# A two-layer GLA and Mamba-2 trunk on one core: 512-column feature products, y before B's and C's convolution, the skip term on ScalarE

## What is computed

```python
proj = h @ w_in
z, xbc, dt = split(proj, [2048, 2048 + 4096])
xbc = silu(conv1d(xbc, conv_w, 4 taps, causal) + conv_b)
x, B, C = split(xbc, [2048, 2048 + 1024])
dt = softplus(dt + dt_bias)
y = y_diag + y_off + d_skip * x      # inside a chunk, from the state, and the skip term
y = y * silu(z)
y = rmsnorm(y by group) @ w_out
```

## Time and profile before

| | us |
|---|---|
| median of 3 runs | 1087.08 (1086.83 to 1087.44) |
| the profiled execution, its own time | 1086.96 |
| its span, first to last instruction | 1085.2 |
| PE busy | 1075.1 (99%) |
| DVE busy | 787.6 (73%) |
| ACT busy | 652.8 (60%) |
| POOL busy | 87.2 (8%) |
| mean granted clock of PE, as a share of full speed | 0.998 |

### The profile page before, as it was taken

One profiled execution on the slowest core, in us unless ns is written; L12 is line 12 of the kernel. 1 busy time (PEld: TensorE's weight loads), 2 busy tenths in 40 slices (PEclk: granted clock), 3 DMA queues, 4 the chain that ended last, 5 costly groups with the idle time before them and its releaser, 6 DMA issues.

```text
span 1085.2 us, 17549 instructions
## 1 busy us (share of the span) xinstructions
PE 1075.1 (99%) x6399; PEld 940.1 (87%) x6399; DVE 787.6 (73%) x1122; ACT 652.8 (60%) x1002; POOL 87.2 (8%) x138
## 2 busy tenths in 40 slices
PE   9999999999999999999999999999999999999997
PEld 7888888899888888888888888899999988888886
DVE  5867667785677666667766767889888888776664
ACT  7645446784676445458454447697777797454453
POOL 3000000011010000000000000153222211000000
PEclk9999999999999999999999999999999999999999
DMA  9864655375357555474655554595555536655531
GB/s 283 296 230 156 206 180 145 107 241 183 121 163 245 193 190 197 155 233 140 232 192 193 177 171 121 173 289 184 187 155 155 170 121 213 238 171 195 196 112 40
DMA packets 162881, 199.30 MB, mean 184 GB/s; under 512 B 6372, under 2 KB 145856, under 8 KB 162832
## 3 DMA queue, kind: packets, MB, share of 16 engines
q1 hardware_dynamic: 160288, 190.86, 53.9%
q0 software_dynamic: 2384, 7.72, 2.1%
q10 hardware_dynamic: 160, 0.08, 0.0%
HBM read 197.56 MB, written 1.08 MB: 183 GB/s over the span
## 4 chain that ended last, share of the span: by engine, by line
PE 92%; ACT 3%; DMA 2%; DVE 2%; issue 1%; SPq 0%; POOL 0%; DVEq 0%; ACTq 0%; POOLq 0%
PE ps L1772 27%; PE ps L1934 24%; PE ps L1948 13%; PE ps L1826 9%; PE ps L1835 6%; PE ps L1738 5%; PE ps L1859 4%; DMA raw<-in_ffn_w_up 1%; PE ps L1798 1%; PE ps L2294 1%; PE ps L2153 0%; ACT exps L882 0%; PE ps L2298 0%; DVE xres L1179 0%; PE ps L1757 0%
## 5 line engine op out<-in xcount | busy, mean ns | idle before, releaser
L1224 DVE TENSOR_TENSOR ws<-raw,ws 128x1024 fp32r<-128x1024 f32 x180 | 213.3, 1222 | 139.7 <-ACT ws L685 139.7
L1772 PE MATMUL ps<-ws,hT 128*128 128x512 f32 x1320 | 314.0, 392 | 0.0
L685 ACT ACTIVATE ws<-raw 128x1024 fp32r<-128x1024 f32 x183 | 184.7, 1053 | 173.2 <-PE ps L1948 160.3
L1772 PEld LDWEIGHTS ps<-ws,hT 128*128 128x128 f32 x1320 | 243.7, 188 | 49.5 <-issue 1.1
L1934 PE MATMUL ps<-xT,ws 128*128 128x512 f32 x1152 | 267.3, 389 | 0.2 <-ACT ws L685 0.2
L1934 PEld LDWEIGHTS ps<-xT,ws 128*128 128x128 f32 x1152 | 216.1, 188 | 45.5 <-ACT ws L685 0.6
L1146 DVE TENSOR_TENSOR ws<-raw,ws 128x2048 fp32r<-128x2048 f32 (+1 forms) x88 | 197.2, 2243 | 27.8 <-ACT ws L599 27.8
L599 ACT ACTIVATE ws<-raw 128x2048 fp32r<-128x2048 f32 x83 | 157.6, 1909 | 2.6 <-PE ps L1772 2.6
L1948 PEld LDWEIGHTS ps<-xT,ws 128*128 128x128 f32 x1152 | 142.6, 192 | 2.5
L1948 PE MATMUL ps<-xT,ws 128*128 128x256 f32 x1152 | 144.1, 283 | 0.0
L1826 PE MATMUL ps<-xT,ws 128*128 128x256 f32 x960 | 119.2, 284 | 0.0
(11 more groups left out here) (263 smaller groups left out, 864.3 us busy)
## 6 DMA issues: line engine op xcount, KB each, us to landing
raw<-in_ffn_w_down SPq DMA_DIRECT2D x88, 512.0 KB, 4.8
raw<-in_ffn_w_gate SPq DMA_DIRECT2D x86, 512.0 KB, 4.0
raw<-in_ffn_w_up SPq DMA_DIRECT2D x86, 512.0 KB, 5.0
raw<-in_ssd_w_in SPq DMA_DIRECT2D x48, 512.0 KB, 4.7
raw<-in_gla_w_in SPq DMA_DIRECT2D x24, 512.0 KB, 4.8
raw<-in_ssd_w_out SPq DMA_DIRECT2D x16, 512.0 KB, 4.3
raw<-in_gla_w_out SPq DMA_DIRECT2D x8, 512.0 KB, 5.5
exps<-cs_rows POOLq DMA_DIRECT2D x8, 512.0 KB, 5.1
```

The lines of the kernel that those rows point to most:

```text
L685: act.activation(ws[:, 0:2, 0, c], raw[:, 0:2, c], ACT.Copy).then_inc(gu_hi, 1)
L1224: dve.tensor_tensor(ws[:, 0:2, 1, c], raw[:, 0:2, c], ws[:, 0:2, 0, c].bitcast(F32), ALU.subtract).then_inc(gu_lo, 1)
L1772: mm = pe.matmul(ps[:, 2 * t + n, :], hT[:, par, j, a, t * P:(t + 1) * P], ws[:, slot, b, off:off + 512], start=(first and j + a + b == 0) ...
```

## The change

For groups 2 to 7 of the SSD mixer the products of P1 and P2 with the high weights take the high and the low tokens in one instruction of 512 columns (`wide_tiles`), so a bank holds two halves; ACT copies 512 columns into a buffer (`halves`) and DVE adds the halves into `feat` (`join`). The skip term `dx` is made by four ACT copies with a scale (`skips`) in steps 1 to 8, and POOL's two instructions go. In steps 2 to 6 DVE computes y ahead of the convolution of B and C, and ACT squares y ahead of their silus. The state's copy follows its product more closely in steps 2 and 7. At the ends of both mixers POOL's two instructions become eight, and ACT copies two blocks of xT ahead of one square. In step 7 DVE makes the low part of the output weights whole, which before lay half in step 7 and half in step 8.

```diff
+        halves = [scr[:, 1, o:o + 512] for o in (512, 1536)]
...
-                if not (isinstance(g, int) and g == 1):
-                    pool.wait_ge(y_out, 2 * (g - 1 + G))
-                for t in range(NT):
-                    pool.tensor_tensor(out=by_head(dx)[:, t], in0=by_head(xtok)[:, t],
-                                       in1=hb[:, 1, hs].rearrange("p (h o) -> p h o", o=1).broadcast_to([P, HPG, HD]),
-                                       op=ALU.mult).then_inc(tok_mul, 1)
...
-                    for c in (slice((NQ - 2) * QW, (NQ - 1) * QW), slice((NQ - 1) * QW, NQ * QW)):
-                        pool.tensor_tensor(ws[:, 0:2, 1, c], raw[:, 0:2, c], ws[:, 0:2, 0, c].bitcast(F32),
-                                           op=ALU.subtract).then_inc(gu_lo, 1)
+                    for q in range(NQ - 2, NQ):
+                        for o in range(0, QW, QW // 4):
+                            c = slice(q * QW + o, q * QW + o + QW // 4)
+                            ins = pool.tensor_tensor(ws[:, 0:2, 1, c], raw[:, 0:2, c], ws[:, 0:2, 0, c].bitcast(F32),
+                                                     op=ALU.subtract)
+                        ins.then_inc(gu_lo, 1)
...
+            def halves_out(slot, count, banks, done, earlier, columns=(0, 1)):
+                for c in columns:
+                    act.wait_ge(tile_mm[slot], count * 2 + c + 1)
+                    if earlier is not None:
+                        act.wait_ge(joined, earlier + c + 1)
+                    act.activation(halves[c], ps[:, banks + c, :], ACT.Copy).then_inc(done, 1)
...
                 if after_mixer:
+                    x_high(b, 0, range(2))
                     post_square(b, 1, 1)
                 if b < NPH:
-                    x_high(b, 0, range(KD // 2))
+                    x_high(b, 0, range(2 if after_mixer else 0, KD // 2))
...
+                    def skips():
+                        if not first:
+                            act.wait_ge(y_out, 2 * (g - 1 + G))
+                        act.wait_ge(tok_out, g - 1 + G + 1)
+                        for h in range(HPG):
+                            c = slice(h * HD, (h + 1) * HD)
+                            ins = act.activation(dx[:, :, c], xtok[:, :, c], ACT.Copy,
+                                                 scale=hb[:, 1, bass.ds((g - 1) * HPG + h, 1)])
+                        ins.then_inc(skipped, 1)
...
+                            halves_out(SLOT_P2, g + n0[SLOT_P2], A, p2_out, 4 * (g - 2), (0,))
+                            skips()
+                            halves_out(SLOT_P2, g + n0[SLOT_P2], A, p2_out, 4 * (g - 2), (1,))
...
                     if first and ssd:
+                        skips()
                         hi(SLOT_P1, g + n0[SLOT_P1] + 1)
                         gate_silu()
...
                         transposed(C)
                         if ssd:
+                            skips()
                             gate_silu()
...
-                    if second:
+                    early = ssd and proj and scan and not ahead
+                    if early:
                         act.wait_ge(y_done, g)
                         squares()
...
+            def join(g, c, count):
+                dve.wait_ge(p1_out if c < 2 else p2_out, count + c % 2 + 1)
+                dve.tensor_tensor(feat[:, c, CONV - 1:], halves[c % 2][:, 0:T], halves[c % 2][:, T:2 * T],
+                                  ALU.add).then_inc(joined, 1)
...
+                    if proj and scan and ssd and not first:
+                        for c in range(2):
+                            join(g, c, c0)
...
                             if ahead:
-                                dve.wait_ge(p2_out, c0 + 2)
-                                convolution(g, 2)
+                                for c in range(2, 4):
+                                    join(g, c, c0)
+                                convolution(g, 2, range(CONV // 2), True)
+                                state_copied()
+                                convolution(g, 2, range(CONV // 2, CONV))
                             if second:
                                 lo(SLOT_P3, g + n0[SLOT_P3])
-                                x_convolved(state_copied)
+                                state_copied()
+                                x_convolved()
                             else:
-                                if tail:
-                                    lo_half(*out_unit(n - 2, n, n0), 1)
-                                state_copied()
+                                if not ahead:
+                                    state_copied()
...
-                        if ssd and not ahead and not first and not second:
-                            dve.wait_ge(p2_out, c0 + 2)
-                            convolution(g, 2)
...
-                            dve.wait_ge(tok_mul, 4 * g)
+                            dve.wait_ge(skipped, g)
...
+                    if ssd and proj and scan and not first and not ahead:
+                        for c in range(2, 4):
+                            join(g, c, c0)
+                        convolution(g, 2, wide=True)
                     if second:
-                        dve.wait_ge(p2_out, c0 + 2)
-                        convolution(g, 2)
                         norm(g, tail)
...
                     if ssd and ahead:
-                        lo_half(*out_unit(g - 1, n, n0), 0)
+                        lo(*out_unit(g - 1, n, n0))
...
+            def wide_tiles(slot, banks, columns=(0, 1), free=None, low=None):
+                for c in columns:
+                    if free is not None:
+                        pe.wait_ge(free[0], free[1] + c + 1)
...
+                    for k in range(KD):
+                        pe.matmul(ps[:, banks + c, :], weights(k, 0), xT[:, k, :, :].rearrange("p a n -> p (a n)"),
+                                  start=(k == 0), stop=False, skip_group_check=True)
+                    if low is not None and c == columns[0]:
+                        pe.wait_ge(lo_done[low[0]], low[1] + 1)
+                    for k in range(KD):
+                        mm = pe.matmul(ps[:, banks + c, 0:T], weights(k, 1), xT[:, k, 0, :], start=False,
+                                       stop=(k == KD - 1), skip_group_check=True)
+                    mm.then_inc(tile_mm[slot], 1)
...
-                            pe.wait_ge(tok_mul, 4 * (g - 1) + 2)
+                            pe.wait_ge(tok_mul, 2 * g)
```

More of the change, by code:

```diff
@@ L983, in body @@
                             act.wait_ge(feat_done, 4 * (g + G))
-                        tiles_out(SLOT_P1, g + n0[SLOT_P1], A,
-                                  [feat[:, c, CONV - 1:] if ssd else ca[:, c, :] for c in range(2)], p1_out)
+                        if scan and ssd and not first:
+                            halves_out(SLOT_P1, g + n0[SLOT_P1], A, p1_out, None if second else 4 * (g - 2) - 2)
+                        else:
+                            tiles_out(SLOT_P1, g + n0[SLOT_P1], A,
+                                      [feat[:, c, CONV - 1:] if ssd else ca[:, c, :] for c in range(2)], p1_out)
                     def transposed(bank):
```

42 lines of the change are left out of this document (23 added, 19 removed).

## The result

The changed kernel takes **1089.84 us** (median of 10 runs, 1089.53 to 1090.97) against 1087.08 us for the kernel before on the same chip: a ratio of 1.0026, 95% interval 1.0018 to 1.0034. It is slower by 0.26%, where I had forecast 1086.5 us and no change, with 1087.9 us as the upper end of my range. The profiled span went from 1085.2 to 1088.3 us.

What follows compares the result with a forecast made beforehand. PE was taken as the bound, busy for 1075.1 of 1085.2 us. The terms -2.57 + 0.87 + 1.1 + 0.6 - 0.58 = -0.6 us gave 1086.5 us, no change; range 1083.9 to 1087.9 us.

Steps and rivals of the forecast that it cites:

- What PE saves: -2.57: PE's product tiles: each of 24 tiles takes 2.77 us instead of 2.88, saving 0.107 us each, 2.57 us in all.
- A step of the loop: Steps 3 to 6: a step takes 25.9 us, DVE's 22.8 us and ACT's work stay hidden, PE remains unbroken.
- rival 3: Loop steps: the second P1 copy is late by 0.2 us in each step, giving 1087.5 us; chance 0.08.
- Step 1 into step 2: +0.87: P1 of step 2: ACT's skip copies delay B's copy by 1.2 us, so PE loses 0.87 us.
- Step 2 into step 3: +1.1: Step 3: ACT's copies queue behind a late convolution; PE waits at two places, 1.1 us together, once; bounds 0.6 and 1.7.
- Steps 7 and 8: +0.6: Step 7's norm stays in time; in step 8 skip copies delay the last transposes; net 0.6 us, bounds 0.3 and 1.2.
- The mixers' ends: -0.6: GLA and SSD ends: PE's waits of 0.26 us for xT and 0.32 us go; bounds 0 and -0.6.
- My own sign for this term: SSD mixer's end: DVE's L1151, which took 1.35 us beside POOL, would take below 0.8 us.
- (1): Steps 1, 2 and 8: ACT and DVE are not late, the saving arrives whole, giving 1083.8 us; chance 0.20.
- (2): Steps 4 to 7: step 3's wait for ACT returns every step at 1.1 us, giving 1090.9 us; chance 0.07.
- (4): Wide products: each takes the time of two narrow ones, 0.240 us, and saves nothing, giving 1089.1 us; chance 0.02.

## Why the prediction was wrong

**What PE saves: -2.57.** The product of 512 columns was right to 1.5% (1.84 us for eight, 0.230 each), but the tile takes 2.80 us (773.81 to 776.61) and the first of P2, behind the transposes, 2.88. A step saves 0.34 us in its four tiles, 0.085 each instead of 0.107: 2.0 us in all, 0.5 less than my term. By the spacing that the Trainium skill gives (TensorE: Matmul & The Clock Gate, "Back-to-back issue gap") my estimate had been 0.5 us. The traces show four times that.

**A step of the loop.** The order came out as worked out (the convolution of B and C ends 1.3 us into the step, 801.19; I said 1.6), the skip copies are free there, and DVE fits with 23.0 us. That this is near my 22.8 is partly luck: I took 0.7 us off for `dx`, where the rows that I named give 1.54 (4.00 less 2.46), and new waits beside POOL made up for it. Two sizes were off. The joins of x take 1.69 us beside `xdt` and not 0.72, more than my upper bound of 0.7 for each, and the two instructions behind them 1.92 (1.41 before); in the loop both fall on DVE's idle time and cost PE nothing. And the second P1 copy was late. I had given it a margin of 0.24 us, from its end (804.34) to P2 in the chain of waits (804.79), less the 0.21 by which it grows. But in the timeline P2's products begin at 804.54 already; the chain starts a row only where the one before it ends. So there was no margin. That cost 0.08 us a step; I had set it to 0 and made it rival 3. The step is 26.05 instead of 25.9.

**Step 1 into step 2: +0.87.** Right in kind: an idle time of 0.91 us, with the releaser named. The loss is somewhat larger than that. The last tile ahead of P1 begins at 716.69 and P1 at 720.81, 4.12 us later; without the skip copies on ACT (the run with those of step 1 on POOL) the same distance is 3.05 us, so it is 1.07. The reason is the same reading: I let PE arrive by the chain's 716.21, where the timeline has 715.86. **Step 2 into step 3: +1.1.** Right in kind and nearly in size: the step lasts 26.94 us against 26.05, 0.9 more, and it did not come back in the loop. Only one of the two idle times that I named is printed, the one ahead of P2.

**Steps 7 and 8: +0.6.** This step failed. "In step 7 the joins and the whole `lo` (+1.1) fill DVE's idle times and the norm stays in time" looked only at DVE. The whole low part keeps POOL's `xdt` waiting (3.09 us instead of 1.04), and `xdt` in turn keeps DVE's root waiting. The stretch cost 1.28 us where I had 0.17, and the two halves take back 0.63 of that. The part for the skip copies was right in kind: DVE's norm is late by them, but PE waits 0.74 to 0.83 us ahead of the last transposes and not 1.3.

**The mixers' ends: -0.6.** This step failed most: +1.0 measured between the transposes of the two ends. I took one wait of DVE for POOL's piece as the only one ("it waits for a quarter of that"). The runs showed that in a chain of short instructions the next one waits again, for the next piece (0.72 and 0.66 us in a row), and that eight pieces take 0.86 us longer than two instructions. My own sign for this term, that instruction below 0.8 us, came true, and PE was late all the same. With the pieces undone the ends are as long as before, so the gain was not there either. "Bounds 0 and -0.6" left out a loss, and no row excluded one. The Trainium skill (SBUF — State Buffer, "SBUF: two separate sides") has the rule that I had cited: whichever of DVE and POOL starts first keeps the port pair that they share for its whole instruction, and the other waits; on DVE's side it names instructions with two inputs in SBUF and those in its two-port modes. The trace agrees with it: L1180 ends with POOL's piece (309.36 and 309.35), and DVE's root with `xdt` (878.72 and 878.69). By that rule few long instructions are the better choice where a chain of short ones runs beside them; I had the rule and did not follow it down the chain.

**The rivals.** None gives 1089.84 by its own mechanism: PE's saving didn't arrive whole (1), the wait of step 3 was not in every step (2), the late P1 copy was real at 0.4 us in all (3), the products did save (4). The missing rival was that DVE and POOL wait for each other outside the loop.

## What to carry to other kernels

Before an instruction of DVE or POOL is split or made longer, list what the other of the two runs beside it: here a chain of short instructions beside split ones paid a wait for each link, and only one beside a long one. A change that saves on the bounding engine gets its worth only if the parts around it are laid out again and each wait found: here six small edits beside the product tiles were worth 3.9 us, and the tiles 2.0. Where a margin is tenths of a microsecond, read the start from the timeline and not from the chain of waits. Sum the losses where they arise, by the same instruction in both traces, and not by busy time.

## What was not expected of the hardware

- Two DVE instructions on 128x1, 0.22 and 0.16 us alone, took 0.72 and 0.66 in a row beside POOL's pieces; beside two whole POOL instructions the first took 0.57 and the next 0.16.
- Eight POOL instructions of 128x2x256 took 5.62 us, two of 128x2x1024 4.76: 0.86 us for six more instructions, 0.14 each. DVE's turns are not in it: all sixteen pieces of the changed kernel took 0.73 to 0.74 us.
- It goes both ways: POOL's 128x512 product took 1.03 us at the least, and 2.02 or 3.09 according to what DVE ran (the low part in halves or whole); a POOL instruction on 128x2 took 2.51 beside DVE's low part instead of 0.31.
- Two adds of 128x256 on DVE took 0.75 us alone and 1.69 to 2.77 beside POOL.
- A wait of PE of 0.27 us (in the run with y behind the convolution) can be missing from its idle times and show only among the weight loads, or as a longer distance of two marks.
